# Seven adaLN groups of the second layer as sums on VectorE

## What is computed

```python
for l in range(DEPTH):
    last = l == DEPTH - 1
    shift, scale, gate = jnp.split(jax.nn.silu(c) @ ada_w[l] + ada_b[l], 3, axis=-1)
    shift_c, scale_c, gate_c = jnp.split(jax.nn.silu(c_ctx) @ ada_w[l] + ada_b[l], 3, axis=-1)
    h = rmsnorm(x, norm_g[l]) * (1.0 + scale[:, None]) + shift[:, None]
    hc = rmsnorm(xc, norm_g[l]) * (1.0 + scale_c) + shift_c
    ...
    q, k, v, up, uf, g = split_proj(h @ w_in[l])
    ...
    out = merge_branches(att, up, uf, g, pool_w[l], pool_scale[l], fourier_w[l], w_out[l])
    x_new = x + gate[:, None] * out
    if not last:
        ...
        xc = xc + gate_c * outc
```

## Time and profile before

| | |
|---|---|
| median of 3 runs | 2350.83 us (2349.53 to 2353.44) |
| span of the profiled execution | 2348.8 us (it has no time of its own beside the span) |
| TensorE busy | 2272.0 us, 97% |
| VectorE busy | 1288.4 us, 55% |
| ScalarE busy | 1042.1 us, 44% |
| GpSimd busy | 269.0 us, 11% |
| transfers | 437.14 MB, mean 186 GB/s |
| adaLN weight chunks | 192, the last multiplied at 964.5 us |

### The profile page before, as it was taken

One profiled execution on the slowest core, in us unless ns is written; L12 is line 12 of the kernel. 1 busy time (PEld: TensorE's weight loads), 2 busy tenths in 40 slices (PEclk: granted clock), 3 DMA queues, 4 the chain that ended last, 5 costly groups with the idle time before them and its releaser, 6 DMA issues.

```text
span 2348.8 us, 30025 instructions
## 1 busy us (share of the span) xinstructions
PE 2272.0 (97%) x11859; PEld 1830.4 (78%) x11859; DVE 1288.4 (55%) x2030; ACT 1042.1 (44%) x1596; POOL 269.0 (11%) x326
## 2 busy tenths in 40 slices
PE   5899999999999999999999998999999999999998
PEld 2477777777777867678888887888888888888887
DVE  3354523332332264555776776667765777567764
ACT  2233333332322255445554565555544555345553
POOL 1010100000010122100020324111100111001111
PEclk9999999999999999999999998999999999999999
DMA  9974433445655475634566544565655555555553
GB/s 350 341 263 157 149 126 114 139 132 167 243 179 172 134 276 194 237 96 159 181 207 204 172 143 153 179 196 180 189 195 190 187 185 184 198 188 188 188 189 116
DMA packets 322427, 437.14 MB, mean 186 GB/s; under 512 B 13848, under 2 KB 220112, under 8 KB 321264
## 3 DMA queue, kind: packets, MB, share of 16 engines
q1 hardware_dynamic: 316800, 413.19, 53.2%
q0 software_dynamic: 3392, 16.90, 1.9%
q10 hardware_dynamic: 2096, 5.15, 0.6%
HBM read 428.89 MB, written 6.29 MB: 185 GB/s over the span
## 4 chain that ended last, share of the span: by engine, by line
PE 87%; DVE 4%; ACT 3%; DMA 3%; issue 1%; POOL 1%; SPq 0%; ACTq 0%; POOLq 0%
PE ps L1334 24%; PE ps L1335 12%; PE ps L1309 9%; PE ps L1311 8%; PE ps L1310 8%; PE ps L1329 5%; PE ps L1330 5%; PE ps L1331 5%; PE ps L1289 3%; PE ps L1383 1%; DVE SPL L1784 1%; ACT SPL L1540 1%; PE ps L1400 1%; DMA RAW<-in_ada_w_dram 1%; PE ps L1390 1%
## 5 line engine op out<-in xcount | busy, mean ns | idle before, releaser
L1784 DVE TENSOR_TENSOR SPL<-RAW,SPL 128x1024 fp32r<-128x1024 f32 x592 | 751.6, 1274 | 598.4 <-ACT SPL L1540 596.1
L1334 PE MATMUL ps<-HS,SPL 128*128 128x512 f32 x2688 | 957.7, 401 | 10.8 <-DVE SPL L1784 7.8
L1540 ACT ACTIVATE SPL<-RAW 128x1024 fp32r<-128x1024 f32 x592 | 622.1, 1055 | 493.2 <-PE ps L1311 170.9
L1335 PE MATMUL ps<-HS,SPL 128*128 128x256 f32 x2688 | 755.3, 281 | 0.0
L1334 PEld LDWEIGHTS ps<-HS,SPL 128*128 128x128 f32 x2688 | 507.7, 189 | 135.4 <-DVE SPL L1784 5.6
L1335 PEld LDWEIGHTS ps<-HS,SPL 128*128 128x128 f32 x2688 | 510.5, 190 | 2.0 <-issue 1.7
L1309 PE MATMUL ps<-SPL,HS 128*128 128x512 f32 x960 | 396.8, 413 | 12.2 <-DVE SPL L1784 5.3
L1311 PE MATMUL ps<-SPL,HS 128*128 128x512 f32 x960 | 377.1, 393 | 0.0
L1310 PE MATMUL ps<-SPL,HS 128*128 128x512 f32 x960 | 376.9, 393 | 0.0
L1309 PEld LDWEIGHTS ps<-SPL,HS 128*128 128x128 f32 x960 | 182.1, 190 | 75.5 <-issue 17.5
L1310 PEld LDWEIGHTS ps<-SPL,HS 128*128 128x128 f32 x960 | 182.3, 190 | 41.8 <-issue 6.3
(11 more groups left out here) (281 smaller groups left out, 1689.3 us busy)
## 6 DMA issues: line engine op xcount, KB each, us to landing
RAW<-in_w_in_dram SPq DMA_DIRECT2D x208, 512.0 KB, 5.7
RAW<-in_ada_w_dram SPq DMA_DIRECT2D x192, 512.0 KB, 4.9
RAW<-in_ffn_w_up_dram SPq DMA_DIRECT2D x192, 512.0 KB, 3.5
RAW<-in_w_out_dram SPq DMA_DIRECT2D x96, 512.0 KB, 4.5
RAW<-in_ffn_w_down_dram SPq DMA_DIRECT2D x96, 512.0 KB, 4.1
x_spill<-XT POOLq DMA_DIRECT2D x2, 2048.0 KB, 15.3
XT<-x_spill POOLq DMA_DIRECT2D x1, 4096.0 KB, 17.4
MM<-in_x_dram ACTq DMA_DIRECT2D x2, 1024.0 KB, 10.8
```

What stands on the lines that cost most here:

```text
L1334: mm(PS[b][:, :], wr, hh, start=k == 0, stop=False, skip_group_check=True)
L1335: m = mm(PS[b][:, 256:512], wl, hh[:, 0:256], start=False, stop=k == KT - 1, skip_group_check=True)
L1540: act(SPL[:, (n - 1) % NSPL, 0, :], raw_of(i), ACT.Copy).then_inc(s_hi, 1)
L1784: tt(w[:, 1, :], raw_of(s["i"]), w[:, 0, :].bitcast(F32), ALU.subtract).then_inc(s_lo, 1)
```

## The change

Seven groups of layer 1 are no longer multiplied on TensorE: shift groups 1, 2 and 3, for both vectors, and the four gate groups, for the first vector only (the only one wanted). VectorE multiplies each row block of a chunk by the vector's column and adds it up in an accumulator of 128x512 (`ada_sum`: 4 instructions a shift chunk, 2 a gate chunk); TensorE then sums an accumulator over the partitions with matmuls against a column of ones (`sum_turn`: 8 or 4 of them a group), and VectorE adds the bias. The accumulators lie in parts of `XT` and `MM` that are free then.

The place in the list changes too: the shift groups' 24 chunks alternate with the last 24 main chunks of layer 0's projections, where 24 adaLN chunks for TensorE stood. The gate groups' 32 chunks stand in layer 0's output stage, behind main chunks 5 to 28, one behind each and two behind every third, beside the 28 adaLN chunks that stay. Layer 1's list has no adaLN chunk any more. The raw places stay eight and the look-ahead stays 5 places, sum chunks included. Three pairs of semaphores are merged into one each.

```diff
+        ACC = [MM[:, 0:2048].rearrange("p (h v c) -> p h v c", h=2, v=2), XT[:, 5120:7168].rearrange("p (h v c) -> p h v c", h=2, v=2)]
...
             while at["taken"] < min(len(queue), at["pos"] + (START_AHEAD if at["pos"] < 72 else at["ahead"])):
                 i = at["taken"]
-                if queue[i].shape:
+                if queue[i].shape == 1:
+                    add_products(i, queue[i])
+                elif queue[i].shape:
...
+        def add_products(i, c):
+            g = c.group
+            put("ada_sum", i=i, kc=c.kc, acc=g.acc, before=at["summed"], last=g.room() if c.kc == 0 else [])
+            at["summed"] += 2 * len(g.acc)
+            after_chunk[i] = (s_acc, at["summed"])
...
                 c = chunks[i]
+                if c.shape == 1:
+                    at["pos"] = i + 1
+                    if c.then:
+                        c.then()
+                    continue
...
+        def ada_sums(l, g, vectors, where, room):
+
+            half = g % 2
+            acc = [ACC[where][:, half, v, :] for v in range(vectors)]
+
+            def after():
+                sums = (s_acc, at["summed"])
+
+                def turn():
+                    s = put("sum_turn", l=l, g=g, acc=acc, sums=sums, after=use(7), out=tick("ada_out_columns"))
+                    acc_last[where, half] = [(s_accT, s["n"])]
+                    ada_ready[l, g] = (s_ada, s["out"])
+                    bank_last[7] = [ada_ready[l, g]]
+                while len(hi) < 8:
+                    hi.append(idle)
+                hi.insert(8, turn)
...
-                    put("back", last=[last, (s_gm, KT), (s_gs, KT)])
+                    put("back", last=[last, (s_accT, 3), (s_gm, KT), (s_gs, KT)])
...
-        left = [c for g in range(8, 12) for c in ada_group(0, g)] + [c for g in range(12) for c in ada_group(1, g)]
+        left = [c for g in range(8, 12) for c in ada_group(0, g)] + [c for g in (0, 4, 5, 6, 7) for c in ada_group(1, g)]
+        shifts1 = [c for g in range(1, 4) for c in ada_sums(1, g, 2, 1, lambda: [(s_fm, 4)])]
+        gates1 = [c for g in range(8, 12) for c in ada_sums(1, g, 1, 0, lambda: [(s_m2, KT)])]
...
-        lay_out(main0[0] + mixed(main0[1], left))
-        lay_out(mixed(outs0[:28], left) + outs0[28:])
+        lay_out(main0[0] + mixed(main0[1][:40], left) + [c for pair in zip(main0[1][40:], shifts1) for c in pair])
+        seq, mains = [], 0
+        for c in mixed(outs0[:28], left):
+            seq.append(c)
+            mains += c.shape > 0
+            if c.shape and mains > 4 and gates1:
+                n = 2 if mains % 3 == 0 else 1
+                seq.extend(gates1[:n])
+                del gates1[:n]
+        assert not gates1
+        lay_out(seq + outs0[28:])
         lay_out(left[:FILL])
         del left[:FILL]
-        lay_out(mixed(main1[1], left))
-        lay_out(mixed(outs1, left))
+        lay_out(main1[1])
+        lay_out(outs1)
...
+                elif kind == "sum_turn":
+                    e.wait_ge(*s["sums"])
+                    for b in range(4):
+                        for v, acc in enumerate(s["acc"]):
+                            m = mm(PS[7][:, 2 * b + v:2 * b + v + 1], acc[:, b * 128:(b + 1) * 128], ONES[:, 0:1], start=True, stop=True, skip_group_check=True)
+                    m.then_inc(s_accT, 1)
...
+                elif kind == "ada_sum":
+                    i, kc, vectors = s["i"], s["kc"], len(s["acc"])
+                    for sm, v in new((s_c, 1), *s["last"]):
+                        e.wait_ge(sm, v)
+                    e.wait_ge(s_raw[i % NRAW], 16 * (i // NRAW + 1))
+                    for kk in range(2):
+                        w = raw_of(i)[:, kk * 512:(kk + 1) * 512]
+                        for v, acc in enumerate(s["acc"]):
+                            c = CW[:, 4 * kc + 2 * kk + v:4 * kc + 2 * kk + v + 1]
+                            if kc == 0 and kk == 0:
+                                ts(acc, w, c, None, ALU.mult).then_inc(s_acc, 1)
+                            else:
+                                e.wait_ge(s_acc, s["before"] + vectors * (kk - 1) + v + 1)
+                                stt(acc, w, c, acc, ALU.mult, ALU.add).then_inc(s_acc, 1)
```

More of the change, by code:

```diff
@@ L231, in two_block_program @@
         slots = [(i, []) for i in range(4)]
-        at = {"loaded": 0, "taken": 0, "split": 0, "used": 0, "pos": 0, "ahead": AHEAD}
+        at = {"loaded": 0, "taken": 0, "split": 0, "used": 0, "pos": 0, "ahead": AHEAD, "multiplied": 0, "summed": 0}
+        after_chunk, acc_last = {}, {}
         split_no, chunk_split = {}, {}
@@ L257, in group @@
             aps = fm_aps(W, c0) if form == "fm" else tm_aps(W, c0)
-            cs = [Chunk(g, kc, ap, {"ada": 0, "tm": 2, "fm": 4}[form]) for kc, ap in enumerate(aps)]
+            cs = [Chunk(g, kc, ap, {"ada": 0, "sum": 1, "tm": 2, "fm": 4}[form]) for kc, ap in enumerate(aps)]
             cs[-1].then = then
@@ L266, in load_ahead @@
                 last = []
-                if i >= 0 and queue[i].shape:
-                    if i >= at["taken"]:
+                if i >= 0:
+                    if i >= at["taken" if queue[i].shape else "pos"]:
                         return
[L270 to L274, removed]
+                    last = [(s_lo, split_no[i])] if queue[i].shape > 1 else [after_chunk[i]]
                 put("load", i=at["loaded"], last=last)
@@ L286, in run_ahead @@
                     split_no[i], chunk_split[at["split"]] = at["split"], i
-                    last = [(s_chunk, chunk_split[at["split"] - NSPL] + 1)] if at["split"] > NSPL else []
+                    last = [after_chunk[chunk_split[at["split"] - NSPL]]] if at["split"] > NSPL else []
                     put("split", i=i, last=last)
@@ L338, in run_chunks, with chunk_multiplied @@
                     put("mm", i=i, c=c, inputs=inputs, after=after, banks=range(part * half, (part + 1) * half), end=part == parts - 1, src=c.group.src)
-                at["pos"] = i + 1
-                at["used"] += c.shape > 0
+                chunk_multiplied(i)
                 if c.then:
                     c.then()
+        def chunk_multiplied(i):
+            at["pos"] = i + 1
+            at["multiplied"] += 1
+            after_chunk[i] = multiplied()
+            at["used"] += chunks[i].shape > 0
         def staged(tasks):
@@ L368, in two_block_program @@
         ada_ready, s2_ready = {}, {}
+        def ada_sums(l, g, vectors, where, room):
[11 more added lines that the diff above has]
+                hi.insert(8, turn)
+            cs = group("sum", "ada", I["ada_w"][l, :, :], g * 512, [], after, side=0)
+            cs[0].group.acc, cs[0].group.room = acc, lambda: acc_last.get((where, half)) or room()
+            return cs
         def ada_group(l, g, side=0):
@@ L380, in spread @@
             def spread(slot):
-                s = put("ada_turn", slot=slot, l=l, g=g, after=use(7))
+                s = put("ada_turn", slot=slot, l=l, g=g, after=use(7), out=tick("ada_out_columns"))
                 give(slot, (s_adaT, s["n"]))
-                ada_ready[l, g] = (s_ada, s["n"])
+                ada_ready[l, g] = (s_ada, s["out"])
                 bank_last[7] = [ada_ready[l, g]]
@@ L1422, in tensor @@
                     lv, gi = lay[s["l"]], s["gi"]
-                    for sm, v in new(*s["ready"], (s_dft[s["l"]], 16)):
+                    for sm, v in new(*s["ready"], (s_dft, 16 * (s["l"] + 1))):
                         e.wait_ge(sm, v)
@@ L1432, in tensor @@
                     lv = lay[s["l"]]
-                    for sm, v in new((s_ap[s["l"]], 16 * 5)):
+                    for sm, v in new((s_ap, 16 * 5 * (s["l"] + 1))):
                         e.wait_ge(sm, v)
@@ L1820, in vector @@
                         c = c_norm + 16 * l + 4 * (g - 4)
-                        e.wait_ge(s_ada, n)
+                        e.wait_ge(s_ada, s["out"])
                         stt(S2[:, l, 4 * (g - 4):4 * (g - 3), :], a, 1.0, VV[:, c:c + 4].unsqueeze(2).to_broadcast([P, 4, 2]), ALU.add, ALU.mult).then_inc(s_s2, 1)
+                elif kind == "ada_sum":
[12 more added lines that the diff above has]
+                                stt(acc, w, c, acc, ALU.mult, ALU.add).then_inc(s_acc, 1)
+                elif kind == "sum_turn":
+                    l, g = s["l"], s["g"]
+                    c = c_adb + 48 * l + 4 * g
+                    for sm, v in new((s_col, 3)):
+                        e.wait_ge(sm, v)
+                    e.wait_ge(s_accT, n)
+                    vectors = len(s["acc"])
+                    tt(ADA[:, l, 4 * g:4 * g + 4, 0:vectors], PS[7][:, 0:8].rearrange("p (b v) -> p b v", v=2)[:, :, 0:vectors],
+                       VV[:, c:c + 4].unsqueeze(2).to_broadcast([P, 4, vectors]), ALU.add).then_inc(s_ada, 1)
                 elif kind == "h0":
```

32 lines of the change are left out of this document (17 added, 15 removed).

## The result

The changed kernel is slower. Its median is **2363.74 us** (2358.5 to 2366.49, 5 runs) against 2350.83 (2349.53 to 2353.44, 5 runs, of which the table ahead has three): ratio **1.0054, 95% interval 1.004 to 1.0067**. The forecast of 2334, its range of 2319 to 2352 and its sign were all wrong.

What follows compares the result with a forecast made beforehand. The prediction took TensorE, busy 97% of the span, as the bound: 2348.8 - 12.2 (gate stage) + 1 (attention overlap) + 14.7 (output stage) - 20 (layer 1) = 2332.3, plus 2.0 to the median, say 2334 us; range 2319 to 2352.

Steps and rivals of the forecast that it cites:

- Layer 1 ... Net -20: Layer 1's first 32 main chunks: removing 16 pairs and 4 turns saves 21, plus 4 for a wait, less 5.
- Rival 2: Layer 1 held by tiles, context rows and norms, not TensorE: saves 6 instead of 20, 2348 us; chance 0.12.
- now popped only by main chunks: Layer 1: removed chunks were taken to pop side steps too, so 2 us of the saving were deducted.
- Output stage, +14.7: Layer 0 output stage: added sums and turns cost 14.7 us net, 11 of it from stops at two group borders.
- Gate stage, -11.2: Layer 0 gate stage: removed pairs and turns less new turns give -12.2, overlap with attention +1.
- The price of a multiply-add: VectorE's added 128x512 sums: 0.75 us per instruction, between bounds of 0.48 and 1.27.
- rival 4: VectorE sums: a multiply-add costs 1.27 us like the 1024-wide row, 29 us more, 2363 us; chance 0.04.
- Transfers: Layer 0 output stage: transfer share rises to 0.87 at 289 GB/s, with no time charged for it.
- Rival 3: Layer 0 output stage: every border stops TensorE because chunks load too late, 5.5 us each, 2360 with seven; chance 0.12.
- Rival 1: Layer 0 output stage: no stop at the borders, 11 us less, 2322 with small terms gone too; chance 0.18.
- B: Layer 0 output stage, from TensorE's restart after the gate products to layer 1's first main matmul: forecast +14.7 us.
- D: Layer 1 output, from VectorE's third join of bank rows to the end of that output stage: forecast change 0.

Runs made afterwards that it cites:

- e5: Kernel before, with layer 1's 32 gate chunks left out and layer 0's gates used instead, nothing moved to VectorE: 2349.06 us, ratio 0.9989.
- e7: Changed kernel with two more pairs of side steps popped behind every second of layer 1's first 32 main chunks: 2377.06 us, ratio 1.0109.
- e9: Against e1: scale groups 4 to 6 go to VectorE beside layer 0's output stage, one sum chunk behind each of main chunks 5 to 28: 2332.72 us, 0.9922.
- e2: Changed kernel with the two-sum places moved inside the groups, never at a group's last chunk: 2344.54 us, ratio 0.9975.
- e3: Changed kernel with a look-ahead of 7 places instead of 5 in the output stage, order unchanged: 2341.22 us, ratio 0.9954.
- e1: Changed kernel with only the shift groups on VectorE; the four gate groups return to TensorE in layer 1: 2344.01 us, ratio 0.9968.
- e6: Kernel before, with the matmuls of layer 1's 32 gate chunks issued twice: 2358.58 us, ratio 1.0031.
- e10: e9 with the sums of layer 1's context squares two steps further behind the squares: 2333.78 us, ratio 0.9927.

## Why the prediction was wrong

**The step that failed: "Layer 1 ... Net -20".** It priced 16 pairs and 4 turns at what they occupy TensorE, 21.1 us, and took off 5 for waits met earlier. Measured: -1.9 in the change and -1.9 in e5, where nothing else moves. The earlier trace rows were read as 138 of 143 us busy, so TensorE bound. But the adaLN chunks were part of that busy time: they ran while chains on ScalarE, VectorE and GpSimd were under way (squares and sums of a context row, tiles of h, head norms), and without them TensorE waits for these. The rows gave a hint: 143 us less 21 of fill and 4.7 of idle is 117 of work that had to be there, and in that time VectorE was busy 81 and ScalarE 75. Rival 2, "layer 1 gives little", was this case; its 6 us was the nearest figure, and it had a chance of 0.12. Of the 5 us taken off, 2 were for side work "now popped only by main chunks"; by e7 that premise is false, for it always was. In e5 13.6 of the 21.1 us turned into idle time, 2.2 went to 11 more matmuls at 0.427 in place of 0.227, 1.9 were won, and 3.4 I didn't place. The wait of 2.33 us at the last turn did go as forecast: the phase that holds it took 50.7 us before and 47.6 after. So the stretch beside the chunks, from which 16 us were to come, became 4 us longer instead, and what was won came from behind it. Some of that is attention work that is done one chunk sooner; how much, no run shows.

**Output stage, +14.7: mechanism right, sizes low.** Exactly two stops, at main chunks 12 and 24, and the other long borders clean. Each costs 6.9 to 7.0 beside the turns: 4.6 of wait (3.9 forecast) and 2.4 of slow matmuls (1.6), 13.9 for both where I had 11. The four turns took 0.9 each and not 0.6, 3.6 in place of 2.4. The group with m10 costs 1.4, with a wait of 1.07 us at 664.40, that with m22 0.4 beside its turn, where I had 1 for both, and the last border 0.8 beside its turn where I had 0.3. Sum +20.1.

**Gate stage, -11.2: nearly right.** Two terms were off. The turn of 8 matmuls was read from the earlier trace rows as 0.88 us, but the eight there are the records of four matmuls (`count_back` puts four). TensorE at such a turn in the kernel after:

```profile
582.46 0.39 PE L1381 MATMUL ps<-HS,SPL 128*128 128x512 f32 x1
582.68 1.84 PE L1425 MATMUL ps<-ONES,XT 128*128 128x1 f32 x16
584.38 0.49 PE L1379 MATMUL ps<-HS,SPL 128*128 128x512 f32 x1
```

The next main matmul comes 1.70 us behind the turn's start; with late pace 1.80 in place of 1.0, +1.6 for the two on the path. The overlap with attention cost 1.8 and not 1, mostly one wait of 1.49 us for L1991 at 494.10. Against both stands that the last interval, where I took the wait for L1940 to end unchanged, shortened by 0.9. Together -9.7; measured -9.8.

**The price of a multiply-add was right.** Groups by line, kernel after (busy us, mean ns of one):

```profile
L1894 DVE SCALAR_TENSOR_TENSOR XT<-RAW,CW,XT 128x512 f32<-128x512 f32 x90 | 61.6, 743 | 0.3 <-issue 0.3
...
L1894 DVE SCALAR_TENSOR_TENSOR MM<-RAW,CW,MM 128x512 f32<-128x512 f32 x60 | 49.4, 823 | 2.0
```

0.743 us for the shift chunks' sums, median 0.752 for the gate chunks', against 0.75; rival 4 is out. The gate chunks' longest took 1.67 us: two of them began at 659.06 and 716.97, while GpSimd's L2362 ran for 1.85 us from 658.33 and for 1.58 from 716.50. "SBUF — State Buffer" of the Trainium skill, section "Who interferes with whom", says that a VectorE instruction with two SBUF inputs contends with a GpSimd instruction that reads SBUF, for ports under an exclusive lock. The doubling agrees, and it decided nothing: e9 runs more such sums in that stage (96 for 64) without a stop.

**Transfers** took 0.74 at 254 GB/s in the output stage (634 to 792), not 0.87, and no border but the two stopped. Rival 3 is out. Rival 1, no stop, is what e2 and e3 build: B of 204.7 and 203.5 against 220.2, a gain of 15.5 and 16.7 where the rival had 11.

**D, +2.8, was not thought of.** The same instructions follow each other at another pace. TensorE, before, then after:

```profile
1112.17 0.39 PE L1334 MATMUL ps<-HS,SPL 128*128 128x512 f32 x1
1112.40 0.28 PE L1335 MATMUL ps<-HS,SPL 128*128 128x256 f32 x1
1112.52 0.39 PE L1334 MATMUL ps<-HS,SPL 128*128 128x512 f32 x1
```

```profile
1118.21 0.40 PE L1384 MATMUL ps<-HS,SPL 128*128 128x512 f32 x1
1118.45 0.28 PE L1385 MATMUL ps<-HS,SPL 128*128 128x256 f32 x1
1118.56 0.40 PE L1384 MATMUL ps<-HS,SPL 128*128 128x512 f32 x1
```

A pair of 512 and 256 columns takes 0.347 us before and 0.353 after, 1.9% more by the stage's mean pace, at a granted clock of 1.00 in both. All five kernels that keep adaLN chunks in layer 1 (before, e1, e6, e9, e10) have D = 143.8, all eight without them 146.6. That is an association; what sets the pace stays open.

## What to carry to other kernels

Work that fills gaps on the busiest engine can be nearly free there: before pricing its removal at its duration, subtract the engine's gaps that it covers, or take it out alone and measure (e5: 21 us of work, 1.9 us of time). Move the work that stands where the engine is bound without it, as e9 does, and leave the filler in place. Where a look-ahead is counted in list entries, new entries shorten it in time; count what stands between a chunk and the next one at every border of a group.

## What was not expected of the hardware

- After a wait TensorE runs at 0.427 us a matmul for a stretch that differs: 12 matmuls behind 4.6 us, 7 behind 3.25, at a granted clock of 0.90 to 0.96 in the first three phases of layer 1 against 1.00 where it never waits. The length of the wait alone doesn't tell: behind the same restart of 1.10 us e3 runs eight matmuls at this pace (granted clock 0.72 in 612 to 618) and e2 none. In this kernel a stop of 4.6 us cost 7.0.
- A group of f32 matmuls with one column each against 128x128 weights takes 1.70 us for 8, 0.21 each, and leaves 16 records. The two-vector adaLN matmuls leave two records each too: eight for a pair of chunks.
- The two paces, 0.347 and 0.353 us, occur at full granted clock in other stretches too, and there without regard to the adaLN chunks: at 1600 to 1700 us it was 0.347 before and 0.353 after, but 0.353 in e6, which keeps the chunks, and 0.347 in e2, which doesn't.
